# Rounded high-and-rest products for the per-head sums of a hybrid decoder layer, and an earlier token shift

## The reference

```python
kk = heads(k * k_k)
kk = kk / jnp.maximum(jnp.sqrt(jnp.sum(kk * kk, axis=-1, keepdims=True)), L2_EPS)
...
mean = jnp.mean(y, axis=-1, keepdims=True)
var = jnp.mean(jnp.square(y - mean), axis=-1, keepdims=True)
...
y = y + (jnp.sum(rh * kh * r_k, axis=-1, keepdims=True) * vh).reshape(B, T, D_RWKV)
...
qn = rms_norm(q, q_norm) * (HEAD_DIM ** -0.5)
kn = rms_norm(ka, k_norm)
...
zs_mix = zs + mu_shift.astype(jnp.float32) * (zs_prev - zs)
```

## Time and profile before

| | |
|---|---|
| median of 3 runs | 1474.78 us (1473.46 to 1477.78) |
| span of the profiled execution | 1471.8 us |
| TensorE busy | 1432.0 us, 97% of the span |
| VectorE busy | 691.5 us, 47% |
| ScalarE busy | 514.4 us, 35% |
| GpSimd busy | 579.4 us, 39% |

### The profile page before, as it was taken

How to read it: one execution, slowest core, us unless ns; L and a number is a source line. 1 busy time by engine, 2 the same in 40 slices (tenths; PEclk the granted TensorE clock), 3 DMA queues, 4 the chain that set the end, 5 groups by cost and what they waited for, 6 DMA issues and landing times.

```text
span 1471.8 us, 34271 instructions
## 1 busy us (share of the span) xinstructions
PE 1432.0 (97%) x14670; PEld 1344.3 (91%) x14670; DVE 691.5 (47%) x1447; ACT 514.4 (35%) x856; POOL 579.4 (39%) x740
## 2 busy tenths in 40 slices
PE   4999999999999999999999999999999999899998
PEld 4998999999999899999999999989999899699998
DVE  7117475664847557475664435343353444500000
ACT  6233242422514233242422544434444343322221
POOL 6353241422424134241422434434344443954442
PEclk9999999999999999999999999999999999999999
DMA  5333131311313113131311853735537375345361
GB/s 198 84 91 89 35 94 37 82 53 45 89 38 84 44 45 104 26 98 38 83 52 38 204 134 90 166 94 144 129 95 166 93 170 127 131 130 158 102 165 45
DMA packets 252084, 143.08 MB, mean 97 GB/s; under 512 B 12109, under 2 KB 245006, under 8 KB 251406
## 3 DMA queue, kind: packets, MB, share of 16 engines
q1 hardware_dynamic: 228316, 125.90, 33.6%
q10 hardware_dynamic: 23618, 15.00, 3.5%
HBM read 125.36 MB, written 15.45 MB: 96 GB/s over the span
## 4 chain that ended last, share of the span: by engine, by line
PE 85%; DVE 4%; POOL 3%; ACT 1%; issue 1%; ACTq 0%; DVEq 0%; POOLq 0%
PE acc L483 57%; PE head_banks L929 3%; PE head_banks L934 3%; PE head_banks L919 2%; PE head_banks L871 2%; PE head_banks L1077 1%; PE head_banks L1097 1%; POOL XL L764 1%; PE head_banks L997 1%; PE head_banks L1090 1%; PE head_banks L1046 1%; PE head_banks L986 1%; PE head_banks L838 1%; PE head_banks L967 1%; PE head_banks L886 1%
## 5 line engine op out<-in xcount | busy, mean ns | idle before, releaser
L466 POOL TENSOR_TENSOR WL<-WR,WH 128x256 fp32r<-128x256 f32 (+1 forms) x656 | 507.1, 804 | 858.9 <-ACT WH L456 838.5
L483 PE MATMUL acc<-XH,WH 128*128 128x260 f32 (+1 forms) x2624 | 569.4, 298 | 9.5 <-POOL WL L466 6.9
L483 PE MATMUL acc<-XH,WL 128*128 128x260 f32 (+1 forms) x2624 | 528.5, 283 | 0.0
L483 PE MATMUL acc<-XL,WH 128*128 128x260 f32 (+1 forms) x2624 | 527.7, 283 | 0.0
L483 PEld LDWEIGHTS acc<-XH,WH 128*128 128x128 f32 (+1 forms) x2624 | 404.6, 188 | 39.9 <-issue 28.7
L483 PEld LDWEIGHTS acc<-XL,WH 128*128 128x128 f32 (+1 forms) x2624 | 404.3, 188 | 0.0
L483 PEld LDWEIGHTS acc<-XH,WL 128*128 128x128 f32 (+1 forms) x2624 | 403.7, 188 | 0.0
L456 ACT ACTIVATE WH<-WR 128x1024 fp32r<-128x1024 f32 (+1 forms) x164 | 171.5, 1048 | 121.9 <-PE acc L483 114.6
L491 ACT ACTIVATE AREN<-acc 128x520 f32<-128x520 f32 (+1 forms) x82 | 49.4, 603 | 362.1 <-PE acc L483 354.8
L1929 DVE TENSOR_TENSOR AREN<-head_banks,AREN 128x512 f32<-128x512 f32 x16 | 11.1, 692 | 169.1 <-PE head_banks L1148 169.1
L1723 DVE TENSOR_TENSOR AREN<-AREN,head_banks 128x128 f32<-128x128 f32 x160 | 46.3, 289 | 33.3 <-PE head_banks L929 19.0
(11 more groups left out here) (238 smaller groups left out, 1597.5 us busy)
## 6 DMA issues: line engine op xcount, KB each, us to landing
WR<-in_w_in SPq DMA_DIRECT2D x128, 512.0 KB, 4.1
WR<-in_w_out SPq DMA_DIRECT2D x32, 512.0 KB, 6.9
out<-AREN ACTq DMA_DIRECT2D x32, 256.0 KB, 3.2
AREN<-in_cache_k_win SPq DMA_DIRECT2D x16, 384.0 KB, 8.0
AREN<-in_cache_v_win SPq DMA_DIRECT2D x16, 384.0 KB, 8.9
mix_scratch<-AREN ACTq DMA_DIRECT2D x16, 260.0 KB, 4.2
AREN<-in_x_prompt SPq DMA_DIRECT2D x4, 1024.0 KB, 7.6
AREN<-in_cache_k_win SPq DMA_DIRECT2D x8, 512.0 KB, 6.9
```

Source lines behind the costliest of these rows:

```text
L466: rest = pool.tensor_tensor(WL[:, place, j:j + 2, 0:M], WR[:, k % 4, j:j + 2, 0:M], WH[:, place, j:j + 2, 0:M].bitcast(F32), ALU.subtract)
L483: mm = pe.matmul(acc[0:M, hf, 0:HT], w[:, (4 * g + k) % 3, j, 0:M], x[:, kt, hf * HT:(hf + 1) * HT], start=(kt == 0 and n == 0), stop=(kt ...
```

## The change

Each of the six sums takes its operand in two parts. ScalarE writes the operand once more, rounded to fp32r (`GH`); VectorE or GpSimd subtracts that from the full value into `GLO`; `group_sums` multiplies both with a rounded 0/1 matrix (`BLKR`, or `MEANR` with 1/64) into one accumulator. The matrices are made by ScalarE ahead of the first pair. The rests of the key squares, of the bonus product and of the B squares are made by GpSimd; those of the mean and the variance by VectorE. The `bonus` sum moves behind `vec`, and `BEHIND_A` is changed: `tail` 9 units (7 to 15), `vec` 2, `bonus` 2, `st` 3, `mean` 4. The next pair's differences (`shift`) go ahead of the last state update, its mixing (`mixed`) behind it, both ahead of `yc`. The key squares of the next pair are made behind the squares of the variance. The arena is laid out anew to make room.

```diff
-BEHIND_A = {"lora": 4, "kk": 3, "tail": 5, "bonus": 4, "vec": 4, "g11": 1, "g21": 1, "tokb": 2, "nn23": 4, "dx2b": 2, "dx4b": 2,
+BEHIND_A = {"lora": 4, "kk": 3, "tail": 9, "vec": 2, "bonus": 2, "g11": 1, "g21": 1, "tokb": 2, "nn23": 4, "dx2b": 2, "dx4b": 2,
...
-            f"y{NC - 1}": 2, "st": 2, "mean": 3}
+            f"y{NC - 1}": 2, "st": 3, "mean": 4}
...
+        def group_sums(pe, weights, slot, bank):
+
+            for hf in range(2):
+                for n, x in enumerate((GH, GLO)):
+                    mm = pe.matmul(HB[:, bank + hf, 0:HT], weights[:, :], x[:, slot, hf * HT:(hf + 1) * HT],
+                                   start=(n == 0), stop=(n == 1))
+            return mm
...
+                pool.wait_ge(a_ksq, i + 1)
+                pool.tensor_tensor(GLO[:, 0, :], KSQ, GH[:, 0, :].bitcast(F32), ALU.subtract).then_inc(a_krest, 1)
                 feed("lora")
...
+                pool.wait_ge(a_act, ACT_A.at(i, "ph"))
+                pool.tensor_tensor(GLO[:, 1, :], T1, GH[:, 1, :].bitcast(F32), ALU.subtract).then_inc(a_prest, 1)
...
+            def square_rests(i):
+                for j in range(2):
+                    pool.wait_ge(b_sq, 2 * i + j + 1)
+                    rest = pool.tensor_tensor(GLO[:, j, :], SQ[:, j, :], GH[:, j, :].bitcast(F32), ALU.subtract)
+                rest.then_inc(b_srest, 1)
...
             pe.wait_ge(p_act, ACT_P.n)
+            pe.wait_ge(s_groups, 1)
...
                 pe.wait_ge(a_act, ACT_A.at(i, "sga"))
-                for hf in range(2):
-                    mm = pe.matmul(HB[:, hf, 0:HT], blk, KSQ[:, hf * HT:(hf + 1) * HT], start=True, stop=True)
-                mm.then_inc(a_pe, PE_A.one("kk"))
+                pe.wait_ge(a_krest, i + 1)
+                group_sums(pe, BLKR, 0, 0).then_inc(a_pe, PE_A.one("kk"))
...
                 fill("vec")
+                pe.wait_ge(a_act, ACT_A.at(i, "tail"))
+                pe.wait_ge(a_prest, i + 1)
+                group_sums(pe, BLKR, 1, 2).then_inc(a_pe, PE_A.one("bonus"))
+                fill("bonus")
...
-                pe.wait_ge(a_act, ACT_A.at(i, "y"))
...
+                pe.wait_ge(a_yrest, i + 1)
+                group_sums(pe, MEANR, 0, 0).then_inc(a_pe, PE_A.one("mean"))
                 fill("mean")
...
+                pe.wait_ge(a_vrest, i + 1)
+                group_sums(pe, MEANR, 1, 2).then_inc(a_pe, PE_A.one("var"))
...
+            act.activation(BLKR[:, :], blk, ACT.Copy)
+            act.activation(MEANR[:, :], blk, ACT.Copy, scale=1.0 / HD).then_inc(s_groups, 1)
+
+            def key_squares(i):
+
+                act.wait_ge(a_mix, DVE_M.at(i, "mix"))
+                act.activation(KSQ, M3[:, 1], ACT.Square, scale=P_["k_k"])
+                act.activation(GH[:, 0, :], M3[:, 1], ACT.Square, scale=P_["k_k"]).then_inc(a_ksq, 1)
...
+                act.activation(GH[:, 1, :], T1, ACT.Copy).then_inc(a_act, ACT_A.one("ph"))
...
-                feed("bonus")
                 act.wait_ge(a_pe, PE_A.at(i, "vec"))
...
+                feed("bonus")
...
+                state(3)
-
+                if next_shift:
+                    mixed(i + 1)
+
+                dve.wait_ge(a_act, ACT_A.at(i, "y"))
+                dve.tensor_tensor(GLO[:, 0, :], Y, GH[:, 0, :].bitcast(F32), ALU.subtract).then_inc(a_yrest, 1)
                 dve.wait_ge(a_pe, PE_A.at(i, "mean"))
```

More of the change, by code:

```diff
@@ L358, in build @@
         BTS = ba.take(NS)
-        SS_, SP_, SPN = ba.take(NS), ba.take(NS), ba.take(NS)
+        SS_ = ba.take(NS)
+        SPN = SP_
         SE = SS_
@@ L381, in build @@
         last = LEVELS - 1
-        PE_A = Steps(["lora", "kk", "tail", "bonus", "vec", *GRAMS, "tokb", "tokk", "tokv", "nn23",
+        PE_A = Steps(["lora", "kk", "tail", "vec", "bonus", *GRAMS, "tokb", "tokk", "tokv", "nn23",
                       *[x for l in LV if l < last
@@ L725, in pair_a @@
                 pool.tensor_tensor(GG, GG, Z[:, 3, 1:TT + 1], ALU.mult).then_inc(a_pool, POOL_A.one("gate"))
-                for name in ("kk", "tail", "bonus", "vec", *GRAMS):
+                for name in ("kk", "tail"):
                     feed(name)
+                pool.wait_ge(a_act, ACT_A.at(i, "ph"))
+                pool.tensor_tensor(GLO[:, 1, :], T1, GH[:, 1, :].bitcast(F32), ALU.subtract).then_inc(a_prest, 1)
+                for name in ("vec", "bonus", *GRAMS):
+                    feed(name)
+                pool.wait_ge(a_prest, i + 1)
                 pool.wait_ge(a_dve, DVE_A.at(i, "bt"))
@@ L850, in pair_a @@
                 fill("tail")
-                pe.wait_ge(a_dve, DVE_A.at(i, "prod"))
-                pe.wait_ge(a_act, ACT_A.at(i, "tail"))
-                for hf in range(2):
-                    mm = pe.matmul(HB[:, 2 + hf, 0:HT], blk, T1[:, hf * HT:(hf + 1) * HT], start=True, stop=True)
-                mm.then_inc(a_pe, PE_A.one("bonus"))
-                fill("bonus")
                 pe.wait_ge(a_dve, DVE_A.at(i, "kka"))
@@ L1011, in pair_a @@
                 fill("st")
-                pe.wait_ge(a_act, ACT_A.at(i, "y"))
-                for hf in range(2):
-                    mm = pe.matmul(HB[:, hf, 0:HT], blkmean, Y[:, hf * HT:(hf + 1) * HT], start=True, stop=True)
-                mm.then_inc(a_pe, PE_A.one("mean"))
+                pe.wait_ge(a_yrest, i + 1)
+                group_sums(pe, MEANR, 0, 0).then_inc(a_pe, PE_A.one("mean"))
                 fill("mean")
-                pe.wait_ge(a_act, ACT_A.at(i, "ysq"))
-                for hf in range(2):
-                    mm = pe.matmul(HB[:, 2 + hf, 0:HT], blkmean, YSQ[:, hf * HT:(hf + 1) * HT], start=True, stop=True)
-                mm.then_inc(a_pe, PE_A.one("var"))
+                pe.wait_ge(a_vrest, i + 1)
+                group_sums(pe, MEANR, 1, 2).then_inc(a_pe, PE_A.one("var"))
                 fill("var")
@@ L1340, in pair_a @@
                 act.wait_ge(a_dve, DVE_A.at(i, "yc"))
-                act.activation(YSQ, YC, ACT.Square).then_inc(a_act, ACT_A.one("ysq"))
+                act.activation(YSQ, YC, ACT.Square)
+                act.activation(GH[:, 1, :], YC, ACT.Square).then_inc(a_act, ACT_A.one("ysq"))
+                if i < PAIRS - 1:
+                    key_squares(i + 1)
                 feed("mean")
@@ L1371, in squares, with high_squares @@
                 for j in range(2):
-                    sq = act.activation(SQ[:, j, :], ZB[:, j, :], ACT.Square)
-                sq.then_inc(b_sq, 1)
+                    act.activation(SQ[:, j, :], ZB[:, j, :], ACT.Square)
+            def high_squares():
+                for j in range(2):
+                    act.activation(GH[:, j, :], ZB[:, j, :], ACT.Square).then_inc(b_sq, 1)
             pair_a(0, group_a(1), next_a(0))
```

72 lines of the change are left out of this document (47 added, 25 removed).

## The result

| | before | after |
|---|---|---|
| median (runs, lowest to highest) | 1476.23 us (4, 1473.46 to 1477.78) | 1529.57 us (4, 1529.33 to 1531.14) |
| span of the profiled execution | 1471.8 us | 1527.3 us |

The ratio is 1.0364 (95% interval 1.0349 to 1.0379): the changed kernel is 53.3 us slower. The direction was predicted, and the time lies inside the range of 1502 to 1532, but 11 us above the forecast of 1518.5.

What follows compares the result with a forecast made beforehand. TensorE, 85% of the chain, was taken to bound the kernel. A pairs 32.8, ends 0.8 and 2.9, B pairs -6.4 give 30.1; with 13.6 for the clock, 43.7 us more: 1474.8 to 1518.5, range 1502 to 1532.

Steps and rivals of the forecast that it cites:

- The mechanism: Each A pair: ScalarE's evacuation waits for unit 15 ahead of e1, so `vec` waits for KKA and TensorE's clock falls.
- three points that would have made it wrong: e1 starting before the evacuation, waits under 3 us, or the clock row staying at 1.00 while the waits are there.
- The wait: TensorE idle from unit 15's end to `vec` in each of eight A pairs: 5.8 us, ends 5.3 and 6.8.
- the price of AR: VectorE's step AR to KKA within the wait, taken as 1.03 us with GpSimd at work; AR alone 0.69.
- Behind `vec`: Stretch from `vec` to the next `lora`: 0.17 us shorter, mean and variance saving 0.80.
- The clock: Slow clock after each of the eight waits: 1.7 us lost each, 13.6 in all.
- the one counterpart of the earlier trace: TensorE's restart at 30.99 after 5.80 us idle, clock granted 0.50, where 1.7 us were lost.
- the clock stays up: Rival: same wait, but the clock holds or falls only at the end of some waits; 1505 us, chance 0.12.
- The ends: Ends of the A part: +0.8 us at the first `lora`, `ssum` about 2.9 us later at the entrance to B.
- what B saves: B pairs: 16 sums save 0.40 us each, 6.4 us, with nothing new on the chain.
- It costs more: Rival: contention on the chain's first steps or a longer slow clock, 1 to 2 us per pair; 1527 to 1540, chance 0.08.
- The chain is not held by the evacuation: Rival: VectorE has e1 before unit 15, pair length unchanged; 1467 us, chance 0.05 shared with another rival.

Runs made afterwards that it cites:

- e4: Kernel before, only the table changed: units 12 to 15 moved from `bonus` into `tail` (9 units, `vec` 4); 1531.12 us, ratio 1.038.
- e5: e1, and in addition GpSimd makes the low half of unit 9's weights only after KKA; 1490.93 us, ratio 1.0112.
- e1: As a run: changed kernel with ScalarE's evacuation of tile 0 moved behind the exponentials, table untouched; 1509.46 us, ratio 1.0231.
- e8: e5 with GpSimd's bonus rest also behind KKA, 11 units in `tail`, matrices made earlier, VectorE making the first B rests; 1465.74 us, ratio 0.9928.
- e3: Changed kernel with 44 useless rounded matmuls between unit 15 and `vec`, filling TensorE's wait; 1519.13 us, ratio 1.0298.
- e2: Changed kernel with 8 units behind `tail` and 3 behind `vec`, so unit 15 and its evacuation stand behind `vec`; 1515.53 us, ratio 1.0277.
- e7: Changed kernel with table, place of `bonus` and two-part `kk` and `bonus` sums taken back; mean, variance, early shift, B sums kept; 1471.68 us, ratio 0.9978.
- e9: e7 with the rounded matrix made earlier, first B squares' high parts right behind `var`, their rests on VectorE; 1467.4 us, ratio 0.9941.

## Why the prediction was right, and where its terms were off

**The mechanism was right.** e1 stood behind the evacuation, VectorE's KKA released `vec` in all eight pairs, and the clock fell behind each. e4 shows the table alone to be enough. None of the three points that would have made it wrong came true.

**The wait: 6.3, not 5.8 us.** The prediction takes the end of unit 15 as the start of its last matmuls plus 0.24. Counted so, the unit ends here at 216.84 + 0.24 = 217.08, 14.11 us after `lora`, just as forecast, and `vec` starts 6.33 us later. (The profile's 6.16, and the 14.28 above, take the modelled end of the last matmul, 0.17 later.) Step by step in the second pair: unit 15 to the evacuation 0.28 (predicted 0.27), evacuation to e1 0.50 (0.60), e1 to rn's end 2.43 (predicted 2.44), KK 0.76 (0.75), then from AR's start to KKA's 222.66 - 221.12 = 1.54, where the sum had 1.03. The term that was too small is the price of AR. I took the row in which the low half of a weight tile ran beside it (1.11 long), but that half ended at 205.87 + 4.19 = 210.06, 0.56 us after AR's start; beside the rest of the bonus product it lasts 1.62. e5 and e1 have 1.63 and 1.62, e4 and e8 0.69. By the Trainium skill, GPSIMD Engine Reference, Key points, some contention was to be expected for an instruction with two SBUF inputs; the traces agree, and give it different sizes. Between `lora` and `vec` this makes 4.84 us more and not 4.3.

**Behind `vec`: +0.07, not -0.17.** In e3, without the clock's part, that stretch takes 73.02 against 72.95. The mean and variance sums saved less than 0.40 each. TensorE, end of the second pair, around the sum of the mean:

```profile
291.50 0.40 PE L496 MATMUL acc<-XH,WL 128*128 128x260 f32 x2
291.87 0.39 PE L513 MATMUL head_banks<-GH,MEANR 128*128 128x260 f32 x1
292.09 0.28 PE L513 MATMUL head_banks<-GLO,MEANR 128*128 128x260 f32 x1
...
292.45 0.40 PE L496 MATMUL acc<-XH,WH 128*128 128x260 f32 x2
```

The unit ahead steps to 291.50 + 0.24 = 291.74, and the next unit starts at 292.45: the sum costs 0.71 us. The first matmul starts 0.13 late (VectorE's rest ended at 291.11 + 0.70 = 291.81) and takes a step of 0.22, not 0.12. At `var` it was 0.61. The 0.5 us of slack that I had read from the earlier trace rows was used up, and 0.1 more. So these two save about 0.4 us together, where the sum had 0.8 less 0.15. (The 0.88 of an fp32 sum stands, though the prediction describes its reading wrongly: 201.45 is the second pair of matmuls behind the sum, one step after the first, and one step is what was taken off.)

**The clock: 2.0, not 1.7 us a pair.** That is e3's measurement, 3 tenths above the one counterpart of the earlier trace rows. That one row came so near was partly luck: e4's shorter wait cost 2.6. The Trainium skill, TensorE: Matmul & The Clock Gate, Part 1, has a clock that must be earned by activity; behind the eight waits the trace agrees. The rival *the clock stays up* fell.

**The ends.** The first `lora` came 2.8 us later, not 0.8. But the first pair, which before had to wait 1.1 us at `kk`, then took only 94.90 - 90.45 = 4.45 us more and not 6.87, so that the stretch is 0.7 above its forecast. Its chain is the rounding, then the two matrices, one behind the other:

```profile
106.53 1.05 ACT L469 ACTIVATE WH<-WR 128x1024 fp32r<-128x1024 f32 x1
107.48 0.30 ACT L1268 ACTIVATE BLKR<-CA 128x128 fp32r<-128x128 f32 x1
107.68 0.30 ACT L1269 ACTIVATE MEANR<-CA 128x128 fp32r<-128x128 f32 x1
```

At the entrance to B GpSimd's low half and the two rests stood in a row, with TensorE behind them:

```profile
868.51 3.27 POOL L479 TENSOR_TENSOR WL<-WR,WH 128x256 fp32r<-128x256 f32 x4 [9.60 <-ACT WH L469]
871.75 3.08 POOL L764 TENSOR_TENSOR GLO<-AREN,GH 128x520 fp32r<-128x520 f32 x2
```

```profile
875.09 0.36 PE L513 MATMUL head_banks<-GH,MEANR 128*128 128x260 f32 x1 [3.97 <-POOL GLO L764]
```

I had priced the two rests at 2 x 1.22; they last 3.08, and the wait lets the clock fall once more (0.57 granted over the next 3.4 us, 1.5 us lost). That ninth fall wasn't in the sum. It is the larger part of what B saves too little: a B pair is 60.72 us and not 61.5, as forecast, but the first is 62.30.

**The rivals.** *It costs more* covers the time, but only with half of its reasons: contention, on AR and not at the chain's start, and a slightly dearer clock. (By its own 1 to 2 us a pair it ends at 1518.5 + 16 = 1534.5, not at 1540.) *The chain is not held by the evacuation* had its point in the wrong place. I compared the end of unit 15 with gl, but behind gl come another 5.6 to 5.9 us until `vec`. Free of the evacuation, `vec` is ready at gl + 5.6; with gl at 9.7 us behind `lora`, as before, this is 15.3, still 1 us behind TensorE's 14.28, and with gl at 12.45 it is 18.05, as e1 and e2 measured. A second wait was hidden under the first, and the prediction names it nowhere, since it kept VectorE's head of the pair at its old durations although GpSimd had been given a rest (L745, 1.56 us) ahead of the gate product. Before, the gate product ran from 5.70 us behind `lora` and VectorE had gl 0.5 us before the low half began, 9.68 against 10.19. Now the gate product runs from 7.35, beside the step that makes `KP`, the scans begin 0.8 us later, and the last steps up to gl lie beside the low half, which starts at 9.79. Two new steps stand ahead of all this, the rounded square of the key on ScalarE (L1275), behind which the end of the pair before comes later, and its rest L745. e7 takes both back, with the rest of the head part; no run moves one of them alone.

The sum of the misses: six pairs at 6.87 for 5.8 give 6.4 us, the last pair and the entrance 2.4, B 1.7 and 0.6, the first pair 0.7; together 11.8.

## What to carry to other kernels

When a table moves a unit of work, look at what *other* engines do in its name, and where those calls stand in their queues: an evacuation that waits for the unit's end blocks all that stands behind it, and one such call ahead of the critical chain cost this kernel 56 us in e4, where only the table was changed. After finding the wait, ask what would be ready next if it were gone (here VectorE, 2.4 us sooner and no more), and price each engine that runs beside the chain with the very instruction that will run there. And give the new copies and rests at the ends of a stage, where nothing covers them, a place of their own: with that done, e9 is 0.59% faster than the kernel before, where e7 was 0.22%.

## What the runs showed of the hardware

**The clock fell while TensorE was at work.** In e3 the windows from 353 to 359 us have TensorE busy for 6.00 of 6.00 us, at 0.55, 0.50 and 0.50, with no wait above 0.2 us near them. The same in e1, without a wait since 308 us. TensorE's windows there:

```profile
340.00:346.00 6.00, 5.85 (x149) 1.00 0.01 3
346.00:350.00 4.00, 3.82 (x57) 0.74 0.00 0
350.00:354.00 4.00, 4.00 (x26) 0.50 0.02 4
```

Ahead of it stand the chain's short products, of 64 rows and columns and 32 or 64 moving columns. It happened in two of eight pairs in e3 (3.0 us each), in one in e1 (4.1 more than its neighbours), in one in e4 (2.6) and not at all in the changed kernel's profile. What decides it wasn't tried. The four executions of e3 lie 6 us apart (1516.26 to 1522.26), those of the changed kernel 1.8; whether such falls make the difference isn't known, since one execution of each has a trace.

**The cost of a wait isn't in proportion to its length.** Behind `vec` the clock took nothing in most pairs after 2.28 us of idleness (e5), 1.5 us after 3.79 (e1), 2.6 after 4.36 (e4) and 2.0 after 6.16. The same wait can also cost differently: in e2, after 4.49 us, the stretch up to the next `lora` took from 75.2 to 76.7 us, where e3's 73.0 and the unit that e2 has more there (0.72) make 73.7.

**The size of contention depends on the neighbour.** A VectorE instruction of 512 columns with two inputs takes 0.69 us alone, 1.22 to 1.23 with the subtraction of a low weight half beside it all the time (L1663 before, L1698 after), and 1.62 beside the rest of the bonus product, which is shorter than the half but one single instruction; L1691 takes 1.49 beside the gate product, where it took 0.70 before. GpSimd's own time varies too: a rest of 520 columns takes 1.10 us at one place and 1.56 at another (L752, L745).
